# Banded attention on Trainium2: values in stacked fp32r products, meta keys in one product, queries in a ring of four tiles

## What is computed

```
s_meta = einsum('bnqhgd,bkhd->bnhgqk', qb, k_meta) * scale
s_band = einsum('bnqhgd,bnkhd->bnhgqk', qb, k_band) * scale
s_band = where(band_ok, s_band, NEG_INF)
probs  = softmax(concatenate([s_meta, s_band, s_sink]))
o = einsum('bnhgqk,bkhd->bnqhgd', probs[..., :N_META], v_meta)
  + einsum('bnhgqk,bnkhd->bnqhgd', probs[..., N_META:N_META + 3 * BLK], v_band)
```

## Time and profile before

| | us |
|---|---|
| median of 3 runs | 2486.98 (2485.07 to 2487.91) |
| the profiled execution | 2486.42 |
| its span in the trace | 2484.8 |
| TensorE / VectorE / ScalarE / GpSimd busy | 2301.5 / 1860.1 / 1482.0 / 617.0 |
| the banded attention | 282.6 to 417.6 |

### The profile page before, as it was taken

The page is one execution under the profiler, slowest core; times in us unless marked ns, Lnnn a source line. Parts: engine busy times, 40 slices in busy tenths (PEclk is TensorE's granted clock), DMA queues, the critical chain, the costliest instruction groups (busy, mean ns, idle before and its releaser), DMA issues. The chain is left out here.

```text
span 2484.8 us, 35047 instructions
## 1 busy us (share of the span) xinstructions
PE 2301.5 (93%) x10673; PEld 1719.7 (69%) x10674; DVE 1860.1 (75%) x2384; ACT 1482.0 (60%) x1738; POOL 617.0 (25%) x557
## 2 busy tenths in 40 slices
PE   6999699999979858999999999999999999999994
PEld 5778555555538726777777877777777777777773
DVE  4466455999966536888887689797878878889975
ACT  4332354888853426667675567575657656768754
POOL 0133000111101232324143123222223222424332
PEclk9999798999989958999999999999999999999997
DMA  4243712313116367989898679896889778979987
GB/s 158 68 117 103 161 39 84 66 38 69 35 39 156 99 154 239 350 282 360 271 361 268 201 249 358 276 335 228 284 280 321 247 239 271 367 263 358 373 301 248
DMA packets 252127, 541.42 MB, mean 218 GB/s; under 512 B 24753, under 2 KB 56753, under 8 KB 251937
## 3 DMA queue, kind: packets, MB, share of 16 engines
q1 hardware_dynamic: 229842, 483.96, 56.9%
q0 software_dynamic: 22208, 56.49, 10.3%
HBM read 498.06 MB, written 65.39 MB: 227 GB/s over the span
## 5 line engine op out<-in xcount | busy, mean ns | idle before, releaser
L1824 DVE TENSOR_TENSOR wlo<-raw_first,whi 128x2048 fp32r<-128x2048 f32 x259 | 616.3, 2392 | 142.4 <-ACT whi L1709 141.1
L1709 ACT CAST whi<-raw_first 128x2048 fp32r<-128x2048 f32 x259 | 489.0, 1907 | 131.0 <-PE gl_ps L2005 94.8
L2007 PE MATMUL gl_ps<-whi,xt_hi 128*128 128x512 f32 x1056 | 418.8, 397 | 27.8 <-DVE wlo L1824 16.3
L2009 PE MATMUL gl_ps<-whi,xt_lo 128*128 128x512 f32 x1056 | 412.6, 391 | 0.0
L2008 PE MATMUL gl_ps<-wlo,xt_hi 128*128 128x512 f32 x1056 | 412.3, 390 | 0.0
L1824 DVE TENSOR_TENSOR wlo<-raw_later,whi 128x2048 fp32r<-128x2048 f32 x128 | 292.3, 2284 | 61.9 <-ACT whi L1709 61.8
L1709 ACT CAST whi<-raw_later 128x2048 fp32r<-128x2048 f32 x128 | 240.8, 1906 | 66.0 <-PE gl_ps L2005 45.6
L2007 PEld LDWEIGHTS gl_ps<-whi,xt_hi 128*128 128x128 f32 x1056 | 198.9, 188 | 80.5 <-ACT whi L1709 20.2
L2009 PEld LDWEIGHTS gl_ps<-whi,xt_lo 128*128 128x128 f32 x1056 | 198.8, 188 | 42.8
L2008 PEld LDWEIGHTS gl_ps<-wlo,xt_hi 128*128 128x128 f32 x1056 | 199.1, 189 | 39.5
L1628 POOL DMA_INDIRECT xg<-v_dram,idn x67 | 108.3, 1616 | 397.2 <-PE t_ps L1977 315.7
(11 more groups left out here) (276 smaller groups left out, 4168.7 us busy)
## 6 DMA issues: line engine op xcount, KB each, us to landing
raw_first<-in_w_mlp SPq DMA_DIRECT2D x260, 1024.0 KB
raw_later<-in_w_mlp SPq DMA_DIRECT2D x130, 1024.0 KB
k_st<-qk_dram SPq DMA_DIRECT2D x32, 260.0 KB, 7.4
xs<-in_x SPq DMA_DIRECT2D x16, 512.0 KB, 4.8
w_in_raw<-in_w_in SPq DMA_DIRECT2D x32, 256.0 KB
q_st<-qk_dram SPq DMA_DIRECT2D x32, 256.0 KB, 6.6
qk_dram<-qk_hi SPq DMA_DIRECT2D x24, 256.0 KB, 2.4
qk_dram<-qk_lo SPq DMA_DIRECT2D x24, 256.0 KB, 2.8
```

What stands on the lines that cost most here:

```text
L1709: act.copy(whi[:, k % SPL, :], raw(k)).then_inc(hi_done, 1)
L1824: dve.tensor_tensor(wlo[:, k % SPL, :], raw(k), whi[:, k % SPL, :].bitcast(F32), ALU.subtract).then_inc(lo_done, 1)
L2007: pe.matmul(bank, xh[:, half, kc, :], hi, start=start, stop=False, skip_group_check=True)
L2009: return pe.matmul(bank, xl[:, half, kc, :], hi, start=False, stop=stop, skip_group_check=True)
```

## The change

Weights and probabilities of the values product are each split into a high part, rounded to fp32r, and a low part, the rest. `v_both` holds high and low values side by side, 128 columns, so that one product with the high probabilities gives high x high in the upper 64 rows of `o_ps` and low x high in the lower 64; a second product, 64 columns, adds high values x low probabilities. For the meta keys high and low probabilities lie in one tile, 16 rows each at partitions 0 and 32 with zeros between, and one product does all. ScalarE now makes the high part of every chunk, VectorE the low part; ScalarE copies the lower half of the output, VectorE adds the upper half. The order in the three loops changes: two exponentials, high parts of chunks 2 and 3, two exponentials on ScalarE; the low parts of chunks 2 and 3 and the add at the end of VectorE's step. The four multiplications into `mixed` become one. Queries live in a ring of four tiles; their loads for tiles 4 to 7 come in two pieces, each waiting for the scores that free its slots, and the next stage's loads stand behind the first of them.

```diff
--- before.py
+++ after.py
...
 def attend_window(nc, a, v_all, mixed, qk_dram, stacks):
...
-        q_st = sb("qa_st", [P, HQ, SEQ], F32R)
+        LOW = 32
+        RING = 4
+        q_st = sb("qa_st", [P, HQ, RING * P], F32R)
...
-        pt = sb("pta", [P, 2, 4, 512])
+        pt_hi = sb("pta_hi", [P, 5, 512], F32R)
+        pt_lo = sb("pta_lo", [P, 5, 512], F32R)
+        pt_meta = sb("pta_meta", [LOW + N_META, 512], F32R)
+        v_both = sb("va_both", [P, NT, HKV, 2 * DH], F32R)
+        v_meta = sb("va_meta", [LOW + N_META, HKV, 2 * DH], F32R)
...
         pieces = [((0, 2 * P), [(0, 3 * P), (SEQ, KEYS)]), ((2 * P, 4 * P), [(3 * P, 5 * P)]),
-                  ((4 * P, NT * P), [(5 * P, NT * P)])]
-        piece_landed = [sem(f"window_piece{i}") for i in range(3)]
+                  ((4 * P, 6 * P), [(5 * P, NT * P)]), ((6 * P, NT * P), [])]
+        piece_landed = [sem(f"window_piece{i}") for i in range(len(pieces))]
...
-        t_ready, t_copied = sem("ta_ready"), sem("ta_copied")
+        t_ready, t_hi, t_lo = sem("ta_ready"), sem("ta_hi"), sem("ta_lo")
+        cleared, v_hi, v_lo, ot_copied = sem("meta_cleared"), sem("va_hi"), sem("va_lo"), sem("ota_copied")
...
+        slot = lambda u, c: 2 * (u % 2) + c if c < 2 else 4
...
-                    sp.dma_start(q_st[rows, :, q0:q1].bitcast(F32), src).then_inc(piece_landed[i], 16)
+                    at = q0 % (RING * P)
+                    sp.dma_start(q_st[rows, :, at:at + q1 - q0].bitcast(F32), src).then_inc(piece_landed[i], 16)
...
             load_piece(1)
-            load_piece(2)
-            stacks.load_small(sp, a)
-            for h in range(2):
-                stacks.load_head(sp, qk_dram, h)
+            for i in (2, 3):
+                sp.wait_ge(s_ready, G * HKV * (pieces[i][0][1] // P - RING))
+                load_piece(i)
+                if i == 2:
+                    stacks.load_small(sp, a)
+                    for h in range(2):
+                        stacks.load_head(sp, qk_dram, h)
         @block.tensor
         def _(pe):
...
-                    q = q_st[:, g * G + j, t * P:(t + 1) * P]
+                    q = q_st[:, g * G + j, (t % RING) * P:(t % RING + 1) * P]
...
                     if n >= 2:
-                        pe.wait_ge(t_copied, n - 1)
+                        pe.wait_ge(t_lo, n - 1)
                     for j in range(G):
                         ins = pe.transpose(t_ps[0:w, n % 2, j * P:(j + 1) * P], sm[:, u % 2, j, c * P:c * P + w], ident[:, :])
                     ins.then_inc(t_ready, 1)
             def values(u):
                 t, g = u // HKV, u % HKV
-                for c in range(nchunk[u]):
-                    w = P if c < nchunk[u] - 1 else N_META
-                    tile = bands[t][c] if w == P else NT
-                    pe.wait_ge(t_copied, before[u] + c + 1)
-                    if c == 0 and u >= 1:
-                        pe.wait_ge(ot_done, u)
-                    ins = pe.matmul(o_ps[0:DV, :], v_all[0:w, tile, g * DH:(g + 1) * DH], pt[0:w, u % 2, c, :],
-                                    start=(c == 0), stop=(c == nchunk[u] - 1))
-                ins.then_inc(o_ready, 1)
+                if u == 0:
+                    pe.wait_ge(v_lo, 2)
+                if u >= 1:
+                    pe.wait_ge(ot_done, u)
+                for c in range(nchunk[u] - 1):
+                    pe.wait_ge(t_lo, before[u] + c + 1)
+                    v = v_both[:, bands[t][c], g, :]
+                    pe.matmul(o_ps[:, :], v, pt_hi[:, slot(u, c), :], start=(c == 0), stop=False, skip_group_check=True)
+                    pe.matmul(o_ps[0:DV, :], v[:, 0:DH], pt_lo[:, slot(u, c), :], start=False, stop=False, skip_group_check=True)
+                pe.wait_ge(t_lo, before[u + 1])
+                pe.matmul(o_ps[:, :], v_meta[:, g, :], pt_meta[:, :], start=False, stop=True, skip_group_check=True
+                          ).then_inc(o_ready, 1)
...
-        def copy_chunk(op, eng, u, c):
-            n = before[u] + c
-            w = P if c < nchunk[u] - 1 else N_META
-            eng.wait_ge(t_ready, n + 1)
-            if n >= 1:
-                eng.wait_ge(t_copied, n)
-            if u >= 2 and c < 2:
-                eng.wait_ge(o_ready, u - 1)
-            op(pt[0:w, u % 2, c, :], t_ps[0:w, n % 2, :]).then_inc(t_copied, 1)
         @block.vector
         def _(dve):
             step = chained(dve, dve_chain)
+            nothing = sm[0:LOW + N_META, 0, :, :].rearrange("p j w -> p (j w)")
+            dve.memset(nothing, 0.0).then_inc(cleared, 1)
+            dve.wait_ge(cleared, 1)
+            dve.tensor_copy(v_meta[:, :, :].rearrange("p g s -> p (g s)"), nothing[:, 0:2 * HKV * DH]).then_inc(cleared, 1)
+            dve.tensor_copy(pt_meta[:, :], nothing[:, 0:512]).then_inc(cleared, 1)
+            dve.wait_ge(cleared, 3)
+            dve.wait_ge(v_hi, 3)
+            v_heads = v_all[:, 0:NT, 0:HKV * DH].rearrange("p t (g d) -> p t g d", d=DH)
+            dve.tensor_tensor(v_both[:, :, :, DH:2 * DH], v_heads, v_both[:, :, :, 0:DH].bitcast(F32), ALU.subtract
+                              ).then_inc(v_lo, 1)
+            dve.tensor_tensor(v_meta[0:N_META, :, DH:2 * DH],
+                              v_all[0:N_META, NT, 0:HKV * DH].rearrange("p (g d) -> p g d", d=DH),
+                              v_meta[0:N_META, :, 0:DH].bitcast(F32), ALU.subtract).then_inc(v_lo, 1)
+            def low(u, c):
+                n = before[u] + c
+                dve.wait_ge(t_hi, n + 1)
+                if c < nchunk[u] - 1:
+                    dve.tensor_tensor(pt_lo[:, slot(u, c), :], t_ps[:, n % 2, :], pt_hi[:, slot(u, c), :].bitcast(F32), ALU.subtract
+                                      ).then_inc(t_lo, 1)
+                else:
+                    dve.tensor_tensor(pt_meta[LOW:LOW + N_META, :], t_ps[0:N_META, n % 2, :],
+                                      pt_meta[0:N_META, :].bitcast(F32), ALU.subtract).then_inc(t_lo, 1)
...
-                    for c in range(2, nchunk[u]):
-                        copy_chunk(dve.tensor_copy, dve, u, c)
+                    for c in range(2):
+                        low(u, c)
                 if n >= 3:
                     u = n - 3
                     t, g = u // HKV, u % HKV
                     dve.wait_ge(ob_ready, u + 1)
                     dve.wait_ge(rl_done, u + 1)
-                    for j in range(G):
-                        hcol = (g * G + j) * DH
-                        ins = dve.tensor_scalar(mixed[:, t, hcol:hcol + DH], ob_ps[:, j * DV:(j + 1) * DV],
-                                                rl[:, u % 4, j:j + 1], None, ALU.mult)
-                    ins.then_inc(ob_done, 1)
+                    dve.tensor_tensor(mixed[:, t, g * G * DH:(g + 1) * G * DH].rearrange("p (j d) -> p j d", d=DH),
+                                      ob_ps[:, 0:G * DV].rearrange("p (j d) -> p j d", d=DH),
+                                      rl[:, u % 4, :].unsqueeze(2).broadcast_to((P, G, DH)), ALU.mult).then_inc(ob_done, 1)
+                if 1 <= n <= U:
+                    for c in range(2, nchunk[n - 1]):
+                        low(n - 1, c)
+                if 2 <= n <= U + 1:
+                    u = n - 2
+                    dve.wait_ge(ot_copied, u + 1)
+                    dve.tensor_tensor(ot[:, u % 2, :], o_ps[0:DV, :], ot[:, u % 2, :], ALU.add).then_inc(ot_done, 1)
         @block.scalar
         def _(act):
+            def high(u, c):
+                n = before[u] + c
+                act.wait_ge(t_ready, n + 1)
+                kept = 2 if c < 2 else 1
+                if u >= kept:
+                    act.wait_ge(o_ready, u - kept + 1)
+                if c < nchunk[u] - 1:
+                    act.copy(pt_hi[:, slot(u, c), :], t_ps[:, n % 2, :]).then_inc(t_hi, 1)
+                else:
+                    act.copy(pt_meta[0:N_META, :], t_ps[0:N_META, n % 2, :]).then_inc(t_hi, 1)
+            meta_values = v_all[0:N_META, NT, 0:HKV * DH].rearrange("p (g d) -> p g d", d=DH)
+            act.copy(v_both[:, :, :, 0:DH], v_all[:, 0:NT, 0:HKV * DH].rearrange("p t (g d) -> p t g d", d=DH)).then_inc(v_hi, 1)
+            act.wait_ge(cleared, 3)
+            act.copy(v_meta[0:N_META, :, 0:DH], meta_values).then_inc(v_hi, 1)
+            act.copy(v_meta[LOW:LOW + N_META, :, 0:DH], meta_values).then_inc(v_hi, 1)
+            def exponent(n, j):
+                b, w = n % 2, width(n)
+                act.activation(sm[:, b, j, 0:w], sm[:, b, j, 0:w], ACT.Exp, bias=nm[:, b, j:j + 1],
+                               accum_out=ls[:, b, j:j + 1]).then_inc(exp_done, 1)
             for n in range(U + 2):
                 if 1 <= n <= U:
                     for c in range(2):
-                        copy_chunk(act.copy, act, n - 1, c)
+                        high(n - 1, c)
                 if n < U:
-                    b, w = n % 2, width(n)
                     act.wait_ge(nm_done, n + 1)
                     if n >= 2:
```

(14 more changed lines are left out.)

## The result

The changed kernel takes 2497.59 us (median of 20 executions, 2486.61 to 2507.05) against 2485.70 for the kernel before on the same chip (20 executions, 2481.79 to 2487.91): ratio 1.0042, 95% interval 1.0029 to 1.0055. It is slower by 12 us (0.4%), where 7.5 us faster was forecast, and it spreads over 20 us where the kernel before spreads over 6. The profiled execution takes 2500.74 us, its span is 2499.1.

A forecast was written before the change was run, and what follows sets the result against it. TensorE's order of work bounded the banded attention at 8.44 us a period; a chain of waits at 7.77 would replace it. 2486.4 - 8.8 gain + 1.4 for the head = 2479.0 us, range 2471 to 2493.

The forecast's parts named there:

- The bound and the chain: Steady units of banded attention: TensorE stops being the bound; a loop across VectorE, TensorE and ScalarE takes 7.77 us against 8.44.
- The handoffs: Eight handoffs between engines per period, 0.04 to 0.7 us each; rival of dearer ones, 2486 to 2488 us, 10%.
- The loads and the prices at nothing: Banded attention: split query loads for tiles 4 to 7 land in time and cost nothing; the single multiplication into mixed hides.
- The head: Start of the stage: first addition at 301.3 us, plus 1.4 us for the clock rising one to two chunks later.
- The end of the stage: Last units of the banded attention: eleven periods end at 386.8 us, mixed ends at 408.8, against 417.57 today.
- The clock: Rival in the banded attention: TensorE's rests of 1.4 us in every 7.8 lower the clock; 26% mild, 12% many low steps.
- the main case: Banded attention: the chain of waits as worked out sets the period, total 2474 to 2482 us; 45%.
- the rival: Clock falls in the stage: a low step takes 11.6 us against 7.77, 3.8 lost; 26% mild, 12% many low steps.
- the case of a few low steps: Clock rival's mild part: one to three low steps of 12 in the banded attention, 2483 to 2490 us; 26%.

The follow-up runs named there:

- the run with nine warming products: Changed kernel plus nine unread products ahead of the stage, eight behind each unit's values from the third on, and 26 increments: 2485.39 us, ratio 1.0003.
- with the place put back: Changed kernel plus 30 semaphore increments on TensorE ahead of its first wait in the windowed stage: 2489.44 us, ratio 1.0013.
- the kernel before moved there cheaply: Kernel before plus 56 plain fp32 products of 16 by 16 and two increments on TensorE, loop at place 217: 2498.95 us, ratio 1.0060.
- before with a warm head: Kernel before plus fourteen products that nothing reads, ahead of the stage's first scores: 2484.97 us, ratio 0.9990.

## Why the prediction was wrong, step by step

**The bound and the chain: right.** In the steady units TensorE stops being the bound; 7.82 us measured for 7.77. TensorE rests 1.16 to 1.19 us a period (1.4 forecast), the additions wait for the output copy, the exponentials run in two pairs with both high parts between. The handoffs cost what was read. Moving the one link that the chain names as late shortened the period, which a merely matching number would not have shown.

**The loads and the prices at nothing: right.** No wait for a piece of queries stands in the stage; the single multiplication into mixed takes 0.42 us.

**The head: mis-sized by 0.6 us.** The price for a later rise of the clock was put at 1.4 us, on top of the chain's 301.3 for the first addition. The rise moved from about 293.8 to 298.6 (0.54 instead of 0.69 in 283.8 to 300) and the first addition came at 303.3, 2.0 behind the chain's.

**The end of the stage: mis-sized by 4.2 us, over half of it the clock.** From the twelfth addition to the last result I had 408.8 - 386.8 = 22.0 us. The trace has 419.77 - 393.61 = 26.16, and its last 12 us ran at the lower level:

```profile
408.00:420.00 12.00, 8.27 (x26) 4.38 (x26) 4.58 (x10) 2.08 (x4) 0.00 (x0) 0.50 0.00 1
```

What this costs can be read against the run with nine warming products, which has the full clock there. From the first product of the last values to the output copy pass 417.13 - 414.30 = 2.83 us against 410.96 - 409.31 = 1.65, and from the last transposes back to the multiplication 0.72 against 0.50, together 1.4. A gap of 6.31 us is 5.4 in three other traces of the same code, another 0.9. So at least 2.3 of the 4.2 are clock. The other 1.9 are put down to links that I let overlap and that stand one behind the other (values, copy, addition, back, multiplication, twice over); no run separates them. Eleven steady units came to 86.4 us instead of 85.5 without their falls.

**The clock: the step that failed.** I gave the falls 38%, and the main case, which the forecast follows, had the full clock from the head to the end of the stage. Each trace of the changed kernel has two to three units of 9.5 to 10.2 us in which the clock fell, about 2 us lost in each, and the lower level again over the last units. The size was wrong as well: 3.8 us a low step in the rival, 1.97 measured, because a fall lasts some 6 to 7 us, less than a unit, and the chain absorbs part of it. The account of the stage: 410.2 (forecast) + 0.6 (head) + 0.9 (eleven units) + 3.9 (two falls) + 4.2 (the end) = 419.8, the 419.77 of the trace. Of the 9.6 us by which the stage is late at least 6.2 are clock (3.9 and 2.3). The warning was in the rows: the earlier trace rows shows a fall after 1.94 us, and I took shorter rests for open and then for harmless.

**The rest of the program: a step that was missing.** Everything behind the stage was carried over unchanged. In the traced execution it took 12.1 us more: the experts 13.0, with the wait of 12.8 us in them, less 0.9 that the stages ahead of and behind them took up. By the runs on one chip (2492.82 against 2489.44 with the place put back) the wait is worth 3.4 us of the median there; against the 2497.59 of the first set it would be 8, since more of its executions were long (13 of 20 above 2493, 5 of 10 here). The forecast without this wait would still have been wrong by 10 us: 2489.4 for 2479.0, inside the range and on the other side of the kernel before.

**The range.** Its top, 2493, held the case of a few low steps, and that case by itself it did hold (2489.4). What it lacked was any term from outside the stage.

## What to carry to other kernels

Take an engine off the bound and it begins to rest; if it is TensorE, price the rests with the clock, at every one of them, before counting a gain, and see whether short work that nothing reads fills them. In the steady part here it cost nothing; at the end of the stage it did, and on its own it gained nothing. Once a chain across three queues is the bound, look for the link that waits last: here a copy placed ahead of two others in its own queue gave some 11 us, where the change of arithmetic by itself gave none. And when a result moves in a stage that the change leaves alone, count the instructions of the looping engine: the same work, shifted by 30 instructions, can cost 12 us at the first jump back.

## What the runs showed of the hardware

A wait for instructions depends on where a loop lies in the program. At places 217 and 229 of a group of 256 TensorE waited 12.5 to 14.6 us at the loop's first jump back, in five of six traces; at 247, 1, 17 and 47 it did not, in eight. The queue that brings instructions moved 46 or 47 packets in each of the five executions with the wait, and 41 to 43 in each of the nine without it. The Trainium skill ("Runtime: NRT & Kernel Launch", section Instruction fetch mechanics) says that instructions come in blocks of 16 KiB, 256 instructions, and that a taken branch to a block that isn't at hand stalls the engine. The trace agrees with the packet size (six packets, 0.10 MB in the stretch of the wait) and with the stall; the section does not say that the place of the loop decides, and no later jump of the same loop waited. Why one execution has the wait and the next one not, at place 217 (by their times about half in the changed kernel, all six in the kernel before moved there cheaply), stays open, and so does the border between the places.

A semaphore increment on TensorE took about 0.15 us when 226 stood in a row (34.9 us in all).

The granted clock fell to 0.50 around rests of 1.0 to 1.9 us in units of 7.4 to 7.8, and it did not fall in any steady unit whose rest was filled (five kernels, about eleven units each). Not every rest brought a fall. The rest of 1.76 or 1.78 us brought one in all five traces that have it unfilled (the fifth is the run with nine warming products); of the repeated rests of 1.2 us most brought none. The places are not free: in three of four traces of the changed kernel they are the second, seventh and ninth unit, in the fourth the second and tenth. In the cases read closely it fell between 0.6 us ahead of TensorE's first instruction behind the rest (288.1 and 288.67, before with a warm head) and 1.9 us behind it (305.8 and 303.87), so what is slowed is the work after the rest.
